# Five places instead of three for the split weight pieces of the expert stage

## The reference

```
for e in range(N_EXPERTS):
    out = out + combine[..., e:e + 1] * swiglu(h, w1[e], w3[e], w2[e])
```

## Time and profile before

| | |
|---|---|
| median of 3 runs | 1626.28 us |
| the profiled execution | 1627.45 us, its span 1625.6 |
| busy: TensorE, VectorE, ScalarE | 97%, 79%, 65% of the span |
| casts to whi, expert stage (L1726) | 328, 623.9 us, 1916 ns each |
| splits to wlo, expert stage (L2359) | 328, 739.9 us, 2287 ns each |
| expert pieces (L1372) | 336 DMAs of 1024 KB, median 8.0 us to landing |
| granted TensorE clock, mean | 0.994 of full speed |

### The profile page before, as it was taken

One profiled execution on the slowest core, in us unless ns is written; L12 is line 12 of the kernel. 1 busy time (PEld: TensorE's weight loads), 2 busy tenths in 40 slices (PEclk: granted clock), 3 DMA queues, 4 the chain that ended last, 5 costly groups with the idle time before them and its releaser, 6 DMA issues.

```text
span 1625.6 us, 21020 instructions
## 1 busy us (share of the span) xinstructions
PE 1577.1 (97%) x8224; PEld 1336.8 (82%) x8224; DVE 1279.1 (79%) x1204; ACT 1057.5 (65%) x988; POOL 30.5 (2%) x69
## 2 busy tenths in 40 slices
PE   9999999999999999999999999999999999999997
PEld 8988888999989888778877778777788777788885
DVE  6676666555576756688899988899888999888997
ACT  6555445333355554557788877788777888777774
POOL 1000000000000000020000000000000000000100
PEclk9999999999999999999999999999999999999998
DMA  7654478977355535669999999999999999999992
GB/s 234 216 193 143 143 241 277 311 246 228 126 169 173 180 118 182 251 233 423 395 386 421 421 417 386 375 420 420 422 387 393 387 421 421 416 386 367 407 396 116
DMA packets 143112, 497.48 MB, mean 306 GB/s; under 512 B 8534, under 2 KB 64400, under 8 KB 100000
## 3 DMA queue, kind: packets, MB, share of 16 engines
q1 hardware_dynamic: 137008, 479.23, 77.8%
q0 software_dynamic: 2624, 8.45, 1.5%
q10 hardware_dynamic: 3376, 8.39, 1.3%
HBM read 476.64 MB, written 19.40 MB: 305 GB/s over the span
## 4 chain that ended last, share of the span: by engine, by line
PE 73%; DVE 18%; ACT 4%; issue 3%; DMA 1%; ACTq 0%; POOL 0%; SPq 0%; DVEq 0%; POOLq 0%
PE bank L730 22%; PE bank L1187 15%; PE bank L1230 13%; DVE wlo L2359 12%; PE bank L901 9%; PE bank L1191 8%; ACT whi L1726 2%; ACT whi L1493 1%; PE bank L720 1%; DVE wlo L1915 1%; PE bank L1015 1%; PE bank L1210 1%; PE bank L1206 1%; DMA hn<-in_mem 1%; ACT pbuf L1628 0%
## 5 line engine op out<-in xcount | busy, mean ns | idle before, releaser
L2359 DVE TENSOR_TENSOR wlo<-raw,whi 128x2048 fp32r<-128x2048 f32 x328 | 739.9, 2287 | 73.0 <-ACT whi L1726 72.4
L1726 ACT ACTIVATE whi<-raw 128x2048 fp32r<-128x2048 f32 x328 | 623.9, 1916 | 160.2 <-PE bank L1191 83.1
L1915 DVE TENSOR_TENSOR wlo<-raw,whi 128x2048 fp32r<-128x2048 f32 (+3 forms) x121 | 259.3, 2148 | 176.3 <-ACT whi L1493 175.9
L1493 ACT ACTIVATE whi<-raw 128x2048 fp32r<-128x2048 f32 (+3 forms) x121 | 217.7, 1801 | 145.8 <-PE bank L730 103.3
L1187 PE MATMUL bank<-whi,yT_hi 128*128 128x512 f32 x896 | 312.2, 396 | 0.0
L1191 PE MATMUL bank<-wlo,yT_hi 128*128 128x512 f32 x896 | 241.3, 391 | 2.9 <-DVE wlo L1915 2.8
L1187 PE MATMUL bank<-whi,yT_lo 128*128 128x512 f32 x560 | 216.7, 390 | 0.0
L1230 PE MATMUL bank<-whi,yT_hi 128*128 128x512 f32 x448 | 180.2, 402 | 25.7 <-DVE yT_hi L2390 16.4
L1191 PEld LDWEIGHTS bank<-wlo,yT_hi 128*128 128x128 f32 x896 | 168.3, 188 | 39.9 <-DVE wlo L1915 3.2
L1187 PEld LDWEIGHTS bank<-whi,yT_hi 128*128 128x128 f32 x896 | 167.0, 188 | 33.1
L1230 PE MATMUL bank<-wlo,yT_hi 128*128 128x512 f32 x448 | 175.9, 393 | 0.0
(11 more groups left out here) (323 smaller groups left out, 2062.8 us busy)
## 6 DMA issues: line engine op xcount, KB each, us to landing
raw<-in_moe_w SPq DMA_DIRECT2D x336, 1024.0 KB, 8.0
raw<-in_w_in SPq DMA_DIRECT2D x36, 1024.0 KB, 5.3
raw<-in_dense_w SPq DMA_DIRECT2D x30, 1024.0 KB, 6.4
raw<-in_w_br SPq DMA_DIRECT2D x12, 1024.0 KB, 5.0
rows_by_slot<-qxT SPq DMA_DIRECT2D x23, 512.0 KB, 7.0
raw<-in_w_out SPq DMA_DIRECT2D x8, 1024.0 KB, 5.0
raw<-in_w_mkv SPq DMA_DIRECT2D x6, 1024.0 KB, 8.2
cqkv<-rows_by_slot ACTq DMA_DIRECT2D x7, 512.0 KB, 8.5
```

The costliest lines, as they stand in the source:

```text
L1493: nc.scalar.activation(whi[:, m % SPLIT, 0:floats(n)], raw[:, pieces[n][1], 0:floats(n)], ACT.Copy).then_inc(hi_ready, 1)
L1726: nc.scalar.activation(whi[:, (E0 + n) % SPLIT, :], raw[:, n % RAW, :], ACT.Copy).then_inc(hi_ready, 1)
L1915: V.tensor_tensor(wlo[:, m % SPLIT, 0:size], raw[:, pieces[n][1], 0:size], whi[:, m % SPLIT, 0:size].bitcast(F32), ALU.subtract).then_inc( ...
L2359: V.tensor_tensor(wlo[:, s, :], raw[:, n % RAW, :], whi[:, s, :].bitcast(F32), ALU.subtract).then_inc(lo_ready, 1)
```

## The change

It gives the pieces of the expert stage five places instead of three: the three of whi and wlo, mT as the fourth, hT as the fifth. The first eight pieces keep their places. From the ninth on each takes the place that has been held longest. Pieces from number 290 on, 46 before the end, don't use hT. The overflow experts, which don't run with these inputs, keep three. ScalarE's cast now waits until TensorE has used the piece that held the place (e_before), five back in the steady state.

e_room gives the room by five places, or by three where it is asked "near". Near are: the e_lo and e_hi ahead of a light turn's gated block, and the e_lo ahead of the w1 product around light turns. So both engines' orders change. VectorE gets one wait (products) in the last turn, before it writes over what is in hT.

```
+        spare_parts = [[v[:, :, :].rearrange("p k s -> p (k s)") for v in pair] for pair in (mT, hT)]
+        FIRST_SPARE, HT_END = HEAD + EARLY, N_E - PER_E - HEAD
+        e_home, e_before, holds = [], [], {}
+        for n in range(N_E + PER_E):
+            if n < FIRST_SPARE:
+                home = (E0 + n) % SPLIT
+            elif n >= N_E:
+                home = n % SPLIT
+            else:
+                homes = [h for h in range(SPLIT + 2) if h <= SPLIT or n < HT_END]
+                home = min(homes, key=lambda h: holds.get(h, h - 2 * SPLIT))
+            e_home.append(home)
+            e_before.append(n - SPLIT if n >= N_E else holds.get(home))
+            holds[home] = n
+        last_in_hT = max(n for n in range(N_E) if e_home[n] == SPLIT + 1)
...
-        def e_room(phase, kind, n):
+        def held_part(n, part):
+
+            home = e_home[n]
+            return (whi, wlo)[part][:, home, :] if home < SPLIT else spare_parts[home - SPLIT][part]
+
+        def e_room(phase, kind, n, near=False):
...
-            while i < end and marks["item", i - SPLIT][0] < limit:
+            while i < end and marks.get(("item", i - SPLIT if near else e_before[i]), (0, 0))[0] < limit:
...
+                    elif e_before[n] is None:
+                        reached(act, ("out", DEPTH - 1, T - 1, 1))
                     else:
-                        reached(act, ("item", n - SPLIT), j)
-                    nc.scalar.activation(whi[:, (E0 + n) % SPLIT, :], raw[:, n % RAW, :], ACT.Copy).then_inc(hi_ready, 1)
+                        reached(act, ("item", e_before[n]), j)
+                    nc.scalar.activation(held_part(n, 0), raw[:, n % RAW, :], ACT.Copy).then_inc(hi_ready, 1)
...
-                e_lo(min(e_room(phase, "eT", b_), end - 1 if last else end), j)
+                near = phase != "over" and (light[phase] or (b_ == NM - 1 and phase < LAST and light[phase + 1]))
+                e_lo(min(e_room(phase, "eT", b_, near), end - 1 if last else end), j)
...
+                reached(dve, ("item", last_in_hT))
...
-                    e_lo(e_room(phase, "e1", b_), j)
+                    e_lo(e_room(phase, "e1", b_, is_light(phase)), j)
                     hidden_lo(phase, b_ - 1, j)
                     e_lo(e_room(phase, "e3", b_), j)
...
-                e_lo(e_room(p + 1, "e1", 0))
+                e_lo(e_room(p + 1, "e1", 0, light[p] or light[p + 1]))
```

More of the change, by code:

```diff
@@ L1158, in e_mark, with e_part @@
                 mark(ins, ("item", n), *extra, *[(phase,) + i for i in names])
-            def e_part(tile, ready, n, j):
+            def e_part(part, ready, n, j):
                 pe.wait_ge(ready, E0 + n + 1 + PER_E * j)
                 k = 2 if e_items[n][1] == "w2" else 4
-                return tile[:, (E0 + n) % SPLIT, :].rearrange("p (k c) -> p k c", k=k)
+                return held_part(n, part).rearrange("p (k c) -> p k c", k=k)
             def is_light(phase):
@@ L1174, in up @@
                     n = nth_item[phase, kind, b_, half]
-                    w = e_part(whi, hi_ready, n, j)
+                    w = e_part(0, hi_ready, n, j)
                     if is_light(phase):
@@ L1188, in up @@
                                          start=(half + k + a == 0), stop=False)
-                    w = e_part(wlo, lo_ready, n, j)
+                    w = e_part(1, lo_ready, n, j)
                     for k in range(4):
@@ L1222, in down @@
                     last = b_ == NM - 1 and half == 1
-                    w = (e_part(whi, hi_ready, i, j), e_part(wlo, lo_ready, i, j))
+                    w = (e_part(0, hi_ready, i, j), e_part(1, lo_ready, i, j))
                     terms = ((0, 0), (0, 1)) if is_light(phase) else ((0, 0), (1, 0), (0, 1))
@@ L1782, in blocks @@
                     if is_light(phase):
-                        e_hi(e_room(phase, "eT", b_ - 1), j)
+                        e_hi(e_room(phase, "eT", b_ - 1, True))
                         silu_folded(phase, b_ - 1)
@@ L1830, in _ @@
                 if light[p]:
-                    e_hi(e_room(p, "eT", NM - 1))
+                    e_hi(e_room(p, "eT", NM - 1, True))
                     silu_folded(p, NM - 1)
@@ L1834, in _ @@
                 if not light[p]:
-                    e_hi(e_room(p, "eT", NM - 1))
+                    e_hi(e_room(p, "eT", NM - 1, light[p + 1]))
                     hidden_hi(p, NM - 1)
@@ L2356, in e_lo @@
                 for n in range(n_done, end):
-                    s = (E0 + n) % SPLIT
                     dve.wait_ge(hi_ready, E0 + n + 1 + PER_E * j)
-                    V.tensor_tensor(wlo[:, s, :], raw[:, n % RAW, :], whi[:, s, :].bitcast(F32),
+                    V.tensor_tensor(held_part(n, 1), raw[:, n % RAW, :], held_part(n, 0).bitcast(F32),
                                     ALU.subtract).then_inc(lo_ready, 1)
```

## The result

The changed kernel took **1630.14 us** (median of 10 runs, 1626.5 to 1633.77), against 1626.33 of the kernel before beside it (10 runs, 1624.89 to 1627.75): ratio 1.0024, 95% interval 1.0016 to 1.0032. It is slower by 3.8 us, and 1620.3 was predicted, with a range of 1614.0 to 1626.5. The profiled execution took 1633.77 us, span 1632.0. It is the slowest of the ten, so single losses read from it come out larger than in the median.

A forecast was written before the change was run, and what follows sets the result against it. TensorE, busy 97%, was taken as the bound, with VectorE setting the pace in light experts. Terms -9.7 (three light experts), +3.3 (start), +0.4 (transfers) gave -6.0 us, predicting a median of 1620.3 us, range 1614.0 to 1626.5.

The forecast's parts named there:

- Into a light expert: Last heavy down block before a light expert: yT_lo done sooner, TensorE starts at 824.18 instead of 826.02, 1.84 us won.
- The first light blocks: Start of a light expert: VectorE's gated blocks 5.95 us earlier, no stall in the first two, TensorE 4.05 us ahead in total.
- Out of a light expert: End of a light expert: three splits ahead of rows_lo, a new TensorE stall of 2.7 us, leaving 3.2 us won each.
- The start of turn 0: First down block of turn 0: three splits ahead of yT_lo instead of one, 3.1 us lost, 3.3 with slower first matmuls.
- Heavy blocks: Blocks of heavy experts: yT_lo keeps its time, 0.4 us to spare, so zero effect.
- Transfers: Weight pieces in light experts: 0.4 us lost, for the third light expert; ends 0 and 2 us for each of three.
- they have the room ... and the two places let them be issued 5.4 us earlier: Transfers before light experts: average rates leave 7 us in a heavy expert, 6 before the first light one, for a lead.
- The limit of 12.3 us: Light experts: when a piece takes over 12.3 us from issue to landing, ScalarE waits for transfers.
- slower first matmuls: Start of turn 0: the addition that raises the loss there from 3.1 to 3.3 us.
- transfers take half of it: Rival: transfers cost 2 us in each light expert instead of 0.4 in all, 1625.9 us; chance 0.17.
- The slow rival: Rival: transfers build no lead, gated blocks stay as late, both new waits cost 11.1 us, 1637.4 us; chance 0.08.

The follow-up runs named there:

- half_cols: The changed kernel with the w2 transfers of light turns cut to half their bytes, good only for timing: 1624.92 us.
- out_near: The changed kernel with VectorE's old order back at the end of each light turn, rows_lo before the two extra splits: 1625.68 us.
- busy_only: The changed kernel with its four new TensorE stalls filled by 50 extra matmuls whose result is written over: 1624.48 us.
- start_near: The changed kernel with the old order back on VectorE and ScalarE at the start of turn 0: 1626.32 us.
- graded: both_near, with room growing one place a block in turn 0 and ScalarE doing copy_gate and rows_hi before the casts at light turns' ends: 1616.07 us.
- both_near: The changed kernel with the old order back both at the start of turn 0 and at each light turn's end: 1622.14 us.

## Why the prediction was wrong

The places and the order work as described, and most steps are right to some tenths. Two failed: the lead of the transfers, and the price of a stall.

- *Into a light expert*, 1.84 us: the table has 5.84 to 4.01. Right.
- *The first light blocks*, VectorE 5.95 us ahead with the first stall in the third block: 5.82, and the first stall is in the third. Right.
- *Out of a light expert*, a stall of 2.7 us: with the 0.2 us of issue time 3.5, 3.1 and 2.2 in the changed kernel, where late transfers are mixed in. half_cols, without these, has 2.92 of idle time and so 3.1 us in all three. Right in mechanism, 0.4 us short each.
- *The start of turn 0*, 3.1 us: out_near and half_cols, which have the same half clock near 712 as before had, come to 3.30 and 3.37 at the first down product. Right. (The profiled execution of the changed kernel was spared that half clock, so its 4.24 us show as 2.84.)
- *Heavy blocks*, zero: right for the changed kernel (5.84 at 731.56 and at 780.16).
- *Transfers*, 0.4 us: **wrong**. half_cols gives 5.2. The range of "0 and 2 us for each" held it, the value I took didn't. The step that failed is "they have the room ... and the two places let them be issued 5.4 us earlier". In most of turn 1 pieces are issued at the same distance from the stage's first matmul as before (0.02 us apart), and land 1.5 to 2.0 us later; in turn 3 they land 3.3 to 4.3 later. They are earlier only against TensorE, which entered turn 1 with 5.84 us lost. So the room that the average rate of a heavy expert shows wasn't turned into a lead. The limit of 12.3 us itself was about right: the pieces ahead of the late fifth block took 12.2 to 13.0. But the earlier trace rows had a piece near the first light turn's end at 12.4 already, and that turn was given no loss. I also left out the transfer of the next expert's rows, 0.5 MB in the fourth block, 1.2 us at 421 GB/s, just where the lead runs out; its own share wasn't measured.
- *The price of a stall*: **wrong, and in no term of the sum**. "3.1 us lost, 3.3 with the slower first matmuls" prices a stall at its length. busy_only shows 5.7 us more for the four new stalls, since the clock falls to 1.2 GHz behind them. The rows to read were in the trace of before, a clock of 0.66 in 711 to 716 us and matmuls of 0.63 us behind the stall of 2.80 at 712.34, and the "slower first matmuls" were taken for a trifle. The old stalls that the change removes were mostly short enough for the clock to stay, so the trade of many short stalls for four long ones was worse than equal.

Together: 1620.3 + 5.7 + 5.2, less the 0.4 that the forecast had for transfers, is 1630.8, 0.7 over the measured 1630.1. Of the rivals, "transfers take half of it" named one of the two causes at the right size (5.6 us). The slow rival was half right: transfers built up no lead, though they kept their pace of 2.48 us a piece (418 to 424 GB/s in the windows above). But each light turn still won 5.6 to 5.8 us in its first blocks, out of the pieces that lay ready, and this the rival left out.

That the clock falls behind a given stall isn't certain. In the 14 profiled executions it fell at all 11 stalls of the stage of 2.93 us and more, and at 29 of the 51 from 1.82 to 2.92 (behind the 2.91 before 1145.42 in start_near, and not behind the 2.91 before 1369.87). The changed kernel's times spread over 7.3 us, against 2.9 for before, and its fastest run had a mean clock of 0.992 and its slowest 0.988, which fits. What decides in that range stays open. It also wasn't tried whether the rows' transfer, moved to another block, would take the late stalls away.

## What to carry to other kernels

A deeper ring moves work forward only through the order of instructions, and each place where the order moves is a place where something urgent now stands behind one or two long operations: grant the extra room one place at a time, where the engine has slack, and keep what the bottleneck engine waits for ahead of it. Price a stall of TensorE of some 2 us or more at its length plus the half clock that may follow (1.4 us each for the four here, 5.7 in all), so one long stall isn't worth several short ones of the same sum. And read the lead of transfers from the rows, piece by piece: when it is issued, and how long it lies landed before its cast, not from an average rate over a stage. A stock that lies ready can be spent once.

## What the runs showed of the hardware that was not expected

Fifty more matmuls made the kernel 5.7 us faster. Behind the longest stall, the one before 727.39, half clock cost 3.0 us (8.45 against 5.44 for the same 24 matmuls), three quarters of the stall's own length. A stall of 1.82 us (before 893.77, in graded) was enough to bring the clock down once, and one of 1.89 (before 1065.65, in the kernel before), while one of 1.90 (before 842.75) was not; nor were five of 1.99 to 2.80 in both_near, whose clock didn't fall in the stage at all. Writing splits into the buffers mT and hT instead of wlo changed nothing (2.28 us each).
